# A hybrid decoder block with a hierarchical MoE on one core: the order of loads, scatters, sums and PSUM banks at the kernel's end

## The reference, cut to what matters

```python
u2   = rms_norm(h1, g_ffn)
e0, e1, gate0, gate1 = route(u2)                    # top 1 of 4 groups, top 2 of its 8 experts
y_k  = (silu(u2 @ w_gate[e_k]) * (u2 @ w_up[e_k])) @ w_down[e_k]
out  = h1 + gate0 * y_0 + gate1 * y_1               # for each token
```

## Time and profile before

| | us |
|---|---|
| median of 3 runs | 1220.05 |
| lowest, highest | 1212.62, 1222.78 |
| profiled execution, its time | 1223.42 |
| its span, first to last instruction | 1221.7 |
| TensorE (PE) busy | 1136.4 (93%) |
| VectorE (DVE) busy | 631.4 (52%) |
| ScalarE (ACT) busy | 535.9 (44%) |
| GpSimd (POOL) busy | 227.5 (19%) |

### The profile page before, as it was taken

The page is one execution under the profiler, slowest core; times in us unless marked ns, Lnnn a source line. Parts: engine busy times, 40 slices in busy tenths (PEclk is TensorE's granted clock), DMA queues, the critical chain, the costliest instruction groups (busy, mean ns, idle before and its releaser), DMA issues.

```text
span 1221.7 us, 18240 instructions
## 1 busy us (share of the span) xinstructions
PE 1136.4 (93%) x6728; PEld 856.2 (70%) x6728; DVE 631.4 (52%) x914; ACT 535.9 (44%) x813; POOL 227.5 (19%) x262
## 2 busy tenths in 40 slices
PE   6999999999998999999998999999898999988977
PEld 5999988899996667777766776555555555555533
DVE  6433143334335667667567865444555453445537
ACT  7212241044335455555346755454555454444520
POOL 5000001230300121110313413222222221222110
PEclk8999999999999999989999999999999999999999
DMA  9420015523004334331589999999999999999986
GB/s 271 106 70 1 1 35 168 177 107 115 26 1 129 96 90 96 75 87 70 193 357 357 358 362 414 426 411 403 397 402 400 388 387 365 416 395 385 386 361 252
DMA packets 66092, 291.36 MB, mean 238 GB/s; under 512 B 10573, under 2 KB 36221, under 8 KB 53488
## 3 DMA queue, kind: packets, MB, share of 16 engines
q1 hardware_dynamic: 48176, 243.38, 52.7%
q0 software_dynamic: 16560, 42.45, 9.3%
q10 hardware_dynamic: 1296, 4.72, 1.0%
HBM read 269.57 MB, written 37.93 MB: 252 GB/s over the span
## 4 chain that ended last, share of the span: by engine, by line
DMA 23%; PE 19%; issue 3%; ACT 3%; DVE 2%; POOL 1%; POOLq 0%; SPq 0%; ACTq 0%; DVEq 0%
DMA wu<-in_w_up 18%; PE ps L1528 4%; PE ps L1479 3%; PE ps L1481 3%; PE ps L1480 3%; PE ps L1468 2%; ACT wu_high L1901 1%; ACT yb L1972 1%; DMA expert_rows<-yb,idxs 1%; DMA xg<-u_rows,idxg 1%; DMA slot_table<-aux,sloti 1%; DMA end_u<-expert_rows 1%; PE ps L1517 1%; PE ps L1515 1%; PE ps L1516 1%
## 5 line engine op out<-in xcount | busy, mean ns | idle before, releaser
L2397 DVE TENSOR_TENSOR wu_low<-wu,wu_high 128x2048 fp32r<-128x2048 f32 x34 | 76.6, 2289 | 56.9 <-ACT wu_high L1901 56.9
L1901 ACT ACTIVATE wd_high<-wd 128x2048 fp32r<-128x2048 f32 x36 | 66.9, 1905 | 83.2 <-DMA wd<-in_w_down 80.8
L1493 PE MATMUL ps<-wu,xa 128*64 128x512 f32 x224 | 102.1, 598 | 0.0
L1493 PE MATMUL ps<-wg,xa 128*64 128x512 f32 x224 | 102.1, 598 | 0.0
L2397 DVE TENSOR_TENSOR wd_low<-wd,wd_high 128x2048 fp32r<-128x2048 f32 x36 | 81.2, 2288 | 37.0 <-ACT wd_high L1901 36.9
L1901 ACT ACTIVATE wu_high<-wu 128x2048 fp32r<-128x2048 f32 x34 | 63.2, 1907 | 70.5 <-DMA wu<-in_w_up 69.8
L2397 DVE TENSOR_TENSOR wg_low<-wg,wg_high 128x2048 fp32r<-128x2048 f32 x34 | 76.5, 2288 | 17.8 <-ACT wg_high L1901 17.8
L2545 DVE TENSOR_TENSOR hid<-sil,ps 128x512 f32<-128x512 f32 x18 | 12.4, 687 | 131.8 <-PE ps L1481 130.2
L1901 ACT ACTIVATE wg_high<-wg 128x2048 fp32r<-128x2048 f32 x34 | 63.3, 1907 | 27.0 <-DMA wg<-in_w_gate 25.9
L1019 POOL DMA_INDIRECT expert_rows<-yb,idxs x30 | 44.3, 1476 | 159.3 <-ACT yb L1972 136.8
L1528 PE MATMUL ps<-wd,ha 128*64 128x512 f32 x224 | 52.9, 615 | 20.8 <-ACT ha L1966 20.8
(11 more groups left out here) (453 smaller groups left out, 3026.9 us busy)
## 6 DMA issues: line engine op xcount, KB each, us to landing
wg<-in_w_gate SPq DMA_DIRECT2D x32, 2048.0 KB, 17.3
wu<-in_w_up SPq DMA_DIRECT2D x32, 2048.0 KB, 19.5
wd<-in_w_down SPq DMA_DIRECT2D x32, 2048.0 KB, 20.6
u_rows<-u POOLq DMA_DIRECT2D x14, 512.0 KB, 6.2
raw_c<-in_w_in SPq DMA_DIRECT2D x5, 1024.0 KB, 5.6
xin<-in_x SPq DMA_DIRECT2D x8, 512.0 KB, 10.0
zx<-in_x POOLq DMA_DIRECT2D x4, 1024.0 KB, 7.3
conv_part_rows<-zx POOLq DMA_DIRECT2D x16, 256.0 KB, 3.1
```

The lines of the kernel that those rows point to most:

```text
L1493: last = mm(ps[HALF * n:HALF * (n + 1), 7, :], xa[:, k, :], raw[m][:, 1, k, :], start=(k == 0), stop=(k == KT - 1))
L1901: A(flat_half(wh[m][:, :, :], n), flat_half(raw_kf(m, s), n), ACT.Copy).then_inc(w_high[m], 1)
L2397: return V.tensor_tensor(flat_half(wl[m][:, s, :, :], n), flat_half(raw_kf(m, s), n), flat_half(wh[m][:, :, :], n).bitcast(F32), ALU.subtr ...
```

## The change

Five edits, all in the kernel's end:
- SyncE: h1 of the four late tiles is loaded behind all_out, each just ahead of its own tile's y1 and y0.
- GpSimd: the scatter of block last - 1 comes right behind that of block last - 2; the memset and zero transfers follow, then the gathers of end_gates, then the iota.
- TensorE: four pairs of banks, (2, 3), (5, 6), (0, 1), (4, 7), so tile t waits for the add of tile t - 4.
- VectorE: add_last takes the pair's banks; where they are not neighbours (4 and 7) it is two instructions of 512 columns.
- VectorE's order: add_rows(0), add_rows(1), L2642, add_rows(2), L2648, add_last(0), add_rows(3), add_last(1), add_last(2), add_last(3), then add_rows(t) and add_last(t) for t = 4 to 7.

```diff
--- before.py
+++ after.py
@@ -177,6 +177,7 @@
 
 
 BY_PRODUCT = (4, 5, 6, 7)
+END_BANKS = ((2, 3), (5, 6), (0, 1), (4, 7))
 
 FIRST_CHUNKS = [(META - 2, 258), (META + 256, 256), (META + 512, 256), (META + 768, 256)]
 FIRST_PLACE = {"C": [254, 512, 768, 1024], "H": [2560, 2048, 2304, 1536]}
@@ -816,14 +817,14 @@
             for t in range(NT // 2):
                 load_rows(h1t, t, dram_h1)
             load_matrix("d", second, last, 1)
-            for t in range(NT // 2, NT):
-                load_rows(h1t, t, dram_h1)
             sp.wait_ge(done_with["u"][0], last // 2 + 1)
             sp.wait_ge(all_out, 1)
             for t in range(NT):
                 if t == NT // 2:
                     for m in "gu":
                         sp.wait_ge(done_with[m][1], last // 2 + 1)
+                if t >= NT // 2:
+                    load_rows(h1t, t, dram_h1)
                 load_rows(y1, t, ys[T:, :], y1_in if t in BY_PRODUCT else None)
                 load_rows(y0, t, ys[0:T, :])
 
@@ -1062,14 +1063,7 @@
                     free_result(1 - s, i // 2 + s)
             scatter(last - 2, 0, 2 * last + 1)
             free_result(1, earlier)
-            pool.wait_ge(gates_out, 16)
-            pool.wait_ge(end_rows_ready, 5)
-            for s in range(2):
-                pool.sem_inc(pool_pass, 1)
-                nc.gpsimd.indirect_dma_start(
-                    out=end_gates[:, s:s + 1], out_offset=None, in_=dram_gates[:, :],
-                    in_offset=bass.IndirectOffsetOnAxis(ap=gate_at[:, s:s + 1].bitcast(U32), axis=0),
-                    bounds_check=last_row, oob_is_err=False).then_inc(end_gates_in, 16)
+            scatter(last - 1, 1, 2 * last + 2)
             pool.wait_ge(x_turned, last + 1)
             pool.sem_inc(pool_pass, 1)
             nc.gpsimd.memset(xg[:, 0, :], 0.0).then_inc(pool_step, 1)
@@ -1081,9 +1075,16 @@
                     out=ys[:, :], in_=xg[:, 0, :], in_offset=None,
                     out_offset=bass.IndirectOffsetOnAxis(ap=rows_.bitcast(U32), axis=0),
                     bounds_check=last_row, oob_is_err=False).then_inc(rows_zero, 16)
+            pool.wait_ge(gates_out, 16)
+            pool.wait_ge(end_rows_ready, 5)
+            for s in range(2):
+                pool.sem_inc(pool_pass, 1)
+                nc.gpsimd.indirect_dma_start(
+                    out=end_gates[:, s:s + 1], out_offset=None, in_=dram_gates[:, :],
+                    in_offset=bass.IndirectOffsetOnAxis(ap=gate_at[:, s:s + 1].bitcast(U32), axis=0),
+                    bounds_check=last_row, oob_is_err=False).then_inc(end_gates_in, 16)
             nc.gpsimd.iota(token_no[:, :], pattern=[[1, T]], base=0, channel_multiplier=0,
                            allow_small_or_imprecise_dtypes=True).then_inc(end_rows_ready, 1)
-            scatter(last - 1, 1, 2 * last + 2)
             pool.wait_ge(rows_zero, 32)
             for s in range(2):
                 pool.wait_ge(ys_out[s], 16 * (last // 2))
@@ -1595,17 +1596,13 @@
             turn_hidden(last + 1)
             down_half(last + 1, 0)
 
-            def end_bank(t):
-
-                return (2, 5, 0)[t % 3]
-
             def end_large(t):
 
-                if t >= 3:
-                    pe.wait_ge(fin_ready, t - 2)
+                if t >= len(END_BANKS):
+                    pe.wait_ge(fin_ready, t - len(END_BANKS) + 1)
                 for part in large_rows:
                     for j in range(2):
-                        mm(ps[:, end_bank(t) + j, :], token_hot[0][:, P * t:P * (t + 1)], part[:, F * j:F * (j + 1)],
+                        mm(ps[:, END_BANKS[t % len(END_BANKS)][j], :], token_hot[0][:, P * t:P * (t + 1)], part[:, F * j:F * (j + 1)],
                            start=(part is large_rows[0]), stop=False)
 
             def end_small_rows(t):
@@ -1613,7 +1610,7 @@
                 for part in small_rows:
                     for j in range(2):
                         half_rows = slice(HALF * j, HALF * (j + 1))
-                        last_mm = mm(ps[:, end_bank(t) + j, :], token_hot[1][half_rows, P * t:P * (t + 1)],
+                        last_mm = mm(ps[:, END_BANKS[t % len(END_BANKS)][j], :], token_hot[1][half_rows, P * t:P * (t + 1)],
                                      part[half_rows, :], start=False,
                                      stop=(part is small_rows[1] and t not in BY_PRODUCT))
                 if t not in BY_PRODUCT:
@@ -1623,7 +1620,7 @@
 
                 pe.wait_ge(y1_in[t], 32)
                 for j in range(2):
-                    last_mm = mm(ps[:, end_bank(t) + j, :], gate_diag[t][:, :], end_tile(y1, t)[:, F * j:F * (j + 1)],
+                    last_mm = mm(ps[:, END_BANKS[t % len(END_BANKS)][j], :], gate_diag[t][:, :], end_tile(y1, t)[:, F * j:F * (j + 1)],
                                  start=False, stop=True)
                 last_mm.then_inc(end_made, 1)
 
@@ -2628,9 +2625,12 @@
 
             def add_last(t):
                 dve.wait_ge(end_made, t + 1)
-                b = (2, 5, 0)[t % 3]
-                V.tensor_tensor(end_tile(h1t, t), end_tile(h1t, t), big[:, 512 * b:512 * (b + 2)],
-                                ALU.add).then_inc(fin_ready, 1)
+                first, second = END_BANKS[t % len(END_BANKS)]
+                size = second + 1 - first if second == first + 1 else 1
+                for at, b in enumerate((first, second)[:2 // size]):
+                    own = end_tile(h1t, t)[:, F * at:F * (at + size)]
+                    made_rows = V.tensor_tensor(own, own, big[:, 512 * b:512 * (b + size)], ALU.add)
+                made_rows.then_inc(fin_ready, 1)
 
             dve.wait_ge(end_rows_ready, 6)
             dve.wait_ge(done_with["u"][0], last // 2 + 1)
@@ -2638,23 +2638,24 @@
                 V.tensor_scalar(token_hot[s][:, :], token_no[:, :], end_token[:, s:s + 1], None,
                                 ALU.is_equal).then_inc(hot_ready, 1)
             add_rows(0)
+            add_rows(1)
             dve.wait_ge(end_high_ready, 1)
             V.scalar_tensor_tensor(large_rows[1][:, :], big[:, 5 * 512:7 * 512], end_gates[:, 0:1],
                                    large_rows[0][:, :].bitcast(F32), ALU.mult, ALU.subtract).then_inc(y_taken, 1)
-            add_rows(1)
+            add_rows(2)
             dve.wait_ge(end_high_ready, 3)
             for j in range(2):
                 half_rows = slice(HALF * j, HALF * (j + 1))
                 low = V.scalar_tensor_tensor(small_rows[1][half_rows, :], ps[half_rows, j, :], end_gates[half_rows, 1:2],
                                              small_rows[0][half_rows, :].bitcast(F32), ALU.mult, ALU.subtract)
             low.then_inc(y_taken, 1)
-            for t in range(2, NT - 1):
+            add_last(0)
+            add_rows(3)
+            for t in range(1, 4):
+                add_last(t)
+            for t in range(4, NT):
                 add_rows(t)
-                add_last(t - 2)
-            for t in range(NT - 3, NT - 1):
                 add_last(t)
-            add_rows(NT - 1)
-            add_last(NT - 1)
 
 
 # ---- launch: one core; inputs and outputs as the reference has them ----
```

## The result

The changed kernel runs in 1210.59 us (median of 20 runs, 1205.18 to 1218.97) where the kernel before runs in 1219.3 (median of 20, 1212.62 to 1225.47). The ratio, which is not simply the quotient of the two medians (0.9929), is 0.9944, its 95% interval 0.9925 to 0.9963: 4.5 to 9.1 us less. Nine further runs (e9) gave 0.9949 (0.9931 to 0.9966). The profiled execution took 1218.97 with a span of 1217.3; the forecast was 1218.7 and 1217.0, and a median of 1215.3.

The account below looks back on a forecast made before the run. Expert weight loads bound most of the span; in the last 60 us, the lagging DMA engine's in-order queue. Terms -5.1, +2.6, -2.8, +0.2, +0.2 gave -4.9; the timeline's -4.7 was kept: median 1215.3 us, range 1208 to 1222.

Parts of the forecast that it names:

- (a): SyncE's load queue: four late h1 loads no longer precede the first y0 tile, which lands at 1182.2; -5.1 us.
- Rival 2: First y0 tile: the 9.89 us belong to the y load itself, not the queue ahead; -0.5 us, chance 0.12.
- (b): GpSimd: scatter of block last - 1 moved up, all_out at 1176.3 instead of 1177.0; 0 us taken.
- Rival 4: GpSimd's software queue: zero transfers behind the last scatter put all_out at 1182.5; +2.6 us, chance 0.05.
- (c): VectorE's order: TensorE's small rows start 10.7 us behind the first y0 tile instead of 8.04; +2.6 us.
- (d): TensorE's banks: a fourth pair removes the waits of 0.91 and 1.91 us for tiles 3 and 4; -2.8 us.
- the halves: VectorE: adds of tiles 3 and 7 in two instructions take 1.38 us for 1.22, once on the path; +0.16 us.
- The clock, taken as 0: TensorE's small rows: a low clock lasting longer could cost up to +1 us; 0 taken.
- (e): Last loads at the kernel's end: with five outputs let in before it, the last load lands at 1211.3.
- both chains end together: Kernel's end: sums of tile 7, behind the last load, end at 1212.6; TensorE allows the last add at 1212.5.
- Rival 1: Kernel's end: all seven earlier outputs stand before the last load, landing at 1213.9; -2.0 us, chance 0.15.
- Rival 3: Lagging DMA engine: through with wd near 1172, first y0 tile about 1178; -8.8 us, chance 0.10.

Follow-up runs that it names:

- e9: The changed kernel unedited, run and profiled again: ratio to the kernel before 0.9949 (0.9931 to 0.9966).
- e1: The kernel before with one edit, h1 of the four late tiles loaded behind all_out: ratio to the kernel before 0.9959 (0.9928 to 0.9990).
- e2: The changed kernel with h1 of the late tiles loaded ahead of all_out again: ratio to the kernel before 0.9987 (0.9961 to 1.0014).
- e6: The changed kernel with VectorE's low parts moved ahead of their old places, the large one first: ratio to the kernel before 0.9943 (0.9922 to 0.9965).
- e7: As e6, but h1 of the four late tiles not loaded: span minus the last wd's issue 55.3 us, 1 run.
- e3: The changed kernel with GpSimd's old order, scatter of block last - 1 behind the iota: ratio to the kernel before 0.9959 (0.9934 to 0.9985).
- e5: The changed kernel with VectorE's low parts back at their old places: ratio to the kernel before 0.9955 (0.9929 to 0.9982).
- e4: The changed kernel with three pairs of banks again, VectorE's new order kept: ratio to the kernel before 0.9966 (0.9938 to 0.9995).
- e8: The changed kernel with h1 of the four late tiles not loaded: span minus the last wd's issue 58.2 us, 1 run.
- e11: As e5, with each of the twelve late-tile loads cut into 120 and 8 rows: ratio to the kernel before 1.0049 (1.0029 to 1.0068).

## Why the prediction was right

The forecast was -4.7 us, with a median of 1215.3 in a range of 1208 to 1222. The ratio means -6.8 (4.5 to 9.1), so the forecast lies near the small end of what was measured, and the median of 1210.59 near the lower end of the range. That the profiled execution agrees within 0.3 us (span 1217.3 for 1217.0) is in good part luck: wd's issue fell at 1158.25, 0.12 from where the profile before had it, and over the thirteen profiles it lies anywhere within 14 us. No luck is needed for the tail. The forecast's is 1217.0 - 1158.13 = 58.9, and measured are 59.0 and 58.7. Its terms:

- **(a) Four loads out of the way, -5.1.** Right. Measured 1187.30 to 1182.25, -5.05, and 5.4 of tail for this edit alone (e1). Its undoing takes everything back (e2). Rival 2, that the 9.89 us were the y load's own, has fallen: with all_out at 15.5 to 18.9 us behind wd's issue, the first sum is at 23.8 to 24.4 in every kernel with the late rows behind, and at 28.9 to 29.2 in every one with them in front. (In e6 and e7 the first sum stands behind a low part, but the load itself landed at 24.1 and 24.0.)
- **(b) The scatter, 0.** Right for the first sum, by e3; what a later all_out does to the last load stays open. Its landmark was off: all_out was forecast at 1176.3 and came at 1174.2, the second zero transfer taking 9.8 us instead of the 11.8 that it took before. Rival 4 (all_out after 1179.9) didn't occur.
- **(c) VectorE's order, +2.6.** First sum to TensorE's first small rows: 1192.93 - 1182.25 = 10.7, as forecast. With the low parts back (e5) tile 4 starts 3.1 earlier.
- **(d) The banks, -2.8: the size belonged to two edits.** The waits for tiles 3 and 4 went, but the fourth pair by itself removes only 1.01 (e4), 0.85 with the 0.16 of the halves set against it; the rest went with the place of add 0 in the order. The sum of (c) and (d) was right as a sum, and what it says is that these edits return nothing: e1, without them and with both waits (0.90 and 1.91) still there, is no longer than the others that compute the whole result (58.2, for 58.5 to 60.1).
- **The clock, taken as 0, cost 0.4.** TensorE began at 1188.96, and in 1192.9 to 1194.9 the granted clock was still 0.51: 1.2 GHz, where the forecast, by the 3.2 us of before, would have had the higher clock back at about 1192. It began earlier than before and the clock came back no earlier (1194.9 for 1194.6), so from the first small rows to tile 2 were 2.0 us for 1.1. Tile 4 began at 1198.49 instead of 1198.1, and the last add at 1212.92 instead of 1212.5. Other executions went the other way (e3 and e8), so this term is a matter of the execution.
- **(e) The last load, 1211.3.** It came at 1209.6, with 3.5 stores in front and not 5. So the forecast that both chains end together was off: the load had landed 3.3 us before the last add. Rival 1, all seven stores in front, was further off still. The y0 of the late tiles landed at 35.5, 39.3, 44.3 and 51.4 us behind wd's issue, 3.8 apart as forecast and then more. The alternation of loads and stores that "DMA: Bandwidth & Descriptors", section "Queues, rings and completion order", of the Trainium skill describes agrees with the landings of the table: with stores under way the last load comes 3.5 to 5.8 stores' time behind an undisturbed queue in the kernels with all twenty loads and the late rows behind, and e3's last three loads land 2.5 us apart, two slots of 1.27 for each; were loads to keep their lead, all would be near 47.
- **Rival 3** (a smaller lag) didn't occur: wd took 21.2 to 21.8 us to land in every profile.

What stays open: the tail explains 4.6 us (up to 6.1 between the second profiles), while the two measured ratios mean 6.8 and 6.2, each with an interval down to 4.5 and 4.1. The tail is within both, near their edge; whether the stretch in front of it gains a microsecond or two isn't settled, since its own spread is 14 us over the profiles. And which DMA engines lag, and why, no run shows.

## What to carry to other kernels

When a transfer that everything waits for seems long, count what was queued ahead of it: here 5 of 10 us belonged to four loads wanted 15 us later, and moving them was, as far as one profile of each kernel can tell, the whole gain of a five-part change. A landing is that of the slowest engine: look at the busy share while it is awaited, for the other engines may be idle. And profile a kernel twice before a microsecond is explained; here the same code differs by 1.2 us of tail. Where a wait goes after a change of order and a change of buffers together, undo each alone before crediting either. At a kernel's end in which loads and stores share the DMA engines, finishing early work earlier let more stores in ahead of the last load, so once the sum of transfers sets the end, only fewer transfers help (e6 against e7).

## What the runs showed of the hardware that was not expected

- The lag between DMA engines is steady: in all thirteen profiles the last 2 MB load took 21.2 to 21.8 us, and in the two whose stretches were read there is a microsecond before it in which three quarters of the engines' time was idle. In every one of them exactly four of its counts were late, at 16.0 to 21.8 us, and none of the others that the trace has came after 12.2.
- Cutting loads of 128 rows into 120 and 8 took the rate from 409 to 183 and from 406 to 239 GB/s at nearly the same busy share (e11), with 4 KB packets of 337 and 268 ns for 163.
- The same stretch runs at either clock, from one profile to another of nearly the same code: the first pair of small rows took 0.80 us in the changed kernel, 0.79 in its second profile and 0.80 in e4, but 0.50 in e3 and e8, after the same idle time of TensorE (5.2 to 5.4 us).
